# Two transformer blocks in fp32 on one core: the first four products with w_ada move from TensorE to ScalarE and GpSimd

## The reference, cut to what matters

```python
mod = jax.nn.silu(c) @ w_ada + b_ada          # c: (1, 1024), w_ada: (1024, 3072)
shift, scale, gate = jnp.split(mod, 3, axis=-1)
h = rmsnorm(x, norm_g) * (1 + scale[:, None, :]) + shift[:, None, :]
```

## Time and profile before

| what | value |
|---|---|
| median of 3 runs | 1005.55 us |
| the profiled execution | 1005.98 us, span of its core 1004.2 us |
| PE busy | 909.9 us (91%) |
| DVE, ACT, POOL busy | 362.0, 321.0, 116.9 us |
| moved by DMA | 308.62 MB, mean 307 GB/s |
| granted TensorE clock | 0.967 of full speed on average |

### The profile page before, as it was taken

One profiled execution on the slowest core, in us unless ns is written; L12 is line 12 of the kernel. 1 busy time (PEld: TensorE's weight loads), 2 busy tenths in 40 slices (PEclk: granted clock), 3 DMA queues, 4 the chain that ended last, 5 costly groups with the idle time before them and its releaser, 6 DMA issues.

```text
span 1004.2 us, 26158 instructions
## 1 busy us (share of the span) xinstructions
PE 909.9 (91%) x12047; PEld 788.9 (79%) x12047; DVE 362.0 (36%) x740; ACT 321.0 (32%) x554; POOL 116.9 (12%) x78
## 2 busy tenths in 40 slices
PE   7999999999989898987878777779999999999997
PEld 7887789977767676765656556569989999999995
DVE  4356356843111111111111111125334344873475
ACT  5546646631000000000000000125346555554443
POOL 2110021000000000000000000003311112341122
PEclk9999999999999998999899988899999999999998
DMA  8995296899999999999999999999554444455101
GB/s 283 382 348 187 95 347 231 344 426 404 403 426 424 425 424 425 424 424 426 425 425 426 426 426 424 424 357 369 200 213 168 164 175 169 169 184 202 57 1 43
DMA packets 70861, 308.62 MB, mean 307 GB/s; under 512 B 5152, under 2 KB 11728, under 8 KB 58584
## 3 DMA queue, kind: packets, MB, share of 16 engines
q1 hardware_dynamic: 66816, 302.08, 75.7%
q10 hardware_dynamic: 3928, 4.80, 1.4%
HBM read 305.81 MB, written 2.63 MB: 307 GB/s over the span
## 4 chain that ended last, share of the span: by engine, by line
PE 67%; DMA 20%; DVE 4%; issue 3%; ACT 2%; SPq 2%; POOL 1%; another core or an unknown queue 1%; POOLq 0%; DVEq 0%; ACTq 0%
PE bank L789 66%; DMA ring<-in_w 10%; DMA arena<-in_w 10%; SPq L854 2%; DVE arena L1352 1%; DVE wR L1346 1%; DMA ring<-in_w_in 1%; PE bank L1011 1%; DVE arena L1349 1%; POOL wR L2272 1%; DVE arena L1346 0%; ACT wR L1918 0%; DVE hTR L1352 0%; DVE hTR L1346 0%
## 5 line engine op out<-in xcount | busy, mean ns | idle before, releaser
L789 PE MATMUL bank<-hTR,wR 128*128 128x256 f32 x2520 | 314.3, 285 | 4.3 <-DVE hTR L1352 1.6
L789 PE MATMUL bank<-arena 128*32 128x128 f32 (+7 forms) x4378 | 277.9, 324 | 43.2 <-DMA arena<-in_w 27.3
L789 PEld LDWEIGHTS bank<-hTR,wR 128*128 128x128 f32 x2520 | 305.4, 192 | 8.3 <-issue 4.2
L789 PEld LDWEIGHTS bank<-arena 128*32 128x32 f32 (+5 forms) x4378 | 211.2, 142 | 97.7 <-issue 66.6
L1346 DVE TENSOR_TENSOR wR<-ring,wR 128x1024 fp32r<-128x1024 f32 x108 | 136.9, 1274 | 118.0 <-ACT wR L1918 117.7
L1918 ACT ACTIVATE wR<-ring 128x1024 fp32r<-128x1024 f32 x137 | 143.3, 1054 | 91.0 <-PE bank L789 88.3
L789 PE MATMUL bank<-ring,arena 128*32 128x128 f32 (+3 forms) x2352 | 103.7, 319 | 30.9 <-DMA ring<-in_w 22.0
L789 PEld LDWEIGHTS bank<-ring,arena 128*32 128x32 f32 (+1 forms) x2352 | 68.9, 114 | 51.0 <-issue 31.5
L2063 ACT ACTIVATE arena<-bank,small 128x256 f32<-128x256 f32 x32 | 15.1, 473 | 272.2 <-PE bank L789 272.2
L2272 POOL TENSOR_TENSOR wR<-ring,wR 128x1024 fp32r<-128x1024 f32 x29 | 70.7, 2437 | 265.9 <-ACT wR L1918 265.9
L1680 DVE COPY arena<-bank 128x256 f32<-128x256 f32 x32 | 13.6, 425 | 193.4 <-PE bank L789 193.4
(11 more groups left out here) (190 smaller groups left out, 669.3 us busy)
## 6 DMA issues: line engine op xcount, KB each, us to landing
arena<-in_w SPq DMA_DIRECT2D x53, 2048.0 KB, 39.6
ring<-in_w SPq DMA_DIRECT2D x42, 2048.0 KB, 40.1
ring<-in_w_in SPq DMA_DIRECT2D x25, 2048.0 KB, 10.3
ring<-in_w_ada SPq DMA_DIRECT2D x5, 2048.0 KB, 11.2
arena<-in_w_in SPq DMA_DIRECT2D x4, 2048.0 KB, 13.1
ring<-in_w_o_attn SPq DMA_DIRECT2D x2, 2048.0 KB, 8.3
ring<-in_w_out SPq DMA_DIRECT2D x2, 2048.0 KB, 7.9
ring<-in_w_in SPq DMA_DIRECT2D x2, 1024.0 KB, 9.0
```

The source lines that it names most:

```text
L789: return pe.e.matmul(o, l, r, start=start, stop=stop)
```

## The change

For ada0 to ada3 the product is taken apart. ACT multiplies each of the 8 row blocks [128, 512] of a chunk in the ring by its per-partition value of `silu(c)` in place (`ada_scale`, two blocks a step, four steps a chunk). POOL adds the 8 scaled blocks in place, 8 to 4 to 2 to 1 (`ada_add`: three adds of 1024 columns, one of 512 into ACC). PE is left with the sum over partitions (`adac_sum`: 4 matmuls of 128 weight columns with one column of ones), and DVE copies 4 columns. The four matmul steps leave the generator, which now yields 28 times; a wrapper, `with_ada`, appends scale steps after fill steps 4 to 19, adds after steps 8 to 23, sums after steps 13, 17, 21 and 25. A slot is released when its sum in ACC is written (semaphore `adac`). ada4 and ada5 stay as they were.

```diff
@@ fill_first
             for g in range(4):
-                if g in (1, 2):
-                    b = PB.use(("adaw", g - 1), PR.next()).bank
-                    for m in (1, 0):
-                        O1.add("ada", g - 1, m)
-                        yield
-                    for m in (1, 0):
-                        O1.loads.release(f"ada{2 * g - 2 + m}")
                 for c2 in range(2):
...
-                            if c2 == 0 and g in (1, 2):
-                                PB.use(("ada", g - 1), b)
-                                O1.add("ada_sum", g - 1)
                             yield
...
+        def with_ada(tiles):
+
+            for i, _ in enumerate(tiles):
+                if 4 <= i < 20:
+                    O1.add("ada_scale", i // 4 - 1, i % 4)
+                if 8 <= i < 24:
+                    O1.add("ada_add", i // 4 - 2, i % 4)
+                    if i % 4 == 3:
+                        O1.loads.release(f"ada{i // 4 - 2}")
+                if i % 4 == 1 and 12 < i < 28:
+                    PB.use(("adac", i // 4 - 3), PR.next())
+                    O1.add("adac_sum", i // 4 - 3)
+                yield
+
-        fill = fill_first()
+        fill = with_ada(fill_first())
@@ released
+            elif nm in ("ada4", "ada5"):
+                filled(e, U_["adaw", 2])
             elif nm[:3] == "ada":
-                filled(e, U_["adaw", int(nm[3]) // 2])
+                e.wait_ge(s_adac, int(nm[3]) + 1)
@@ PE
+            elif what == "adac_sum":
+                u = U_["adac", a[0]]
+                may_write(pe, u)
+                pe.wait_ge(s_adac, a[0] + 1)
+                for c in range(4):
+                    last = mm(pe, banks[u.bank][:, c:c + 1], ACC[:, 128 * c:128 * c + 128], ones[:, 0:1], True, True)
+                last.then_inc(u.full, 1)
@@ ACT
+                elif what == "ada_scale":
+                    i, part = a
+                    w = view(f"ada{i}")
+                    s.wait_ge(*landed[f"ada{i}"])
+                    s.wait_ge(s_siluc, 1)
+                    for k in (2 * part, 2 * part + 1):
+                        eng.activation(w[:, k, :], w[:, k, :], ACT.Copy, scale=sc0[:, k:k + 1]).then_inc(s_adas, 1)
@@ POOL
+                elif what == "ada_add":
+                    i, part = a
+                    w = view(f"ada{i}")
+                    p.settle()
+                    if part == 3:
+                        if i:
+                            filled(p, U_["adac", i - 1])
+                        eng.tensor_tensor(ACC, w[:, 0, :], w[:, 1, :], ALU.add).then_inc(s_adac, 1)
+                    else:
+                        o, x = ((0, 4), (2, 6), (0, 2))[part]
+                        p.wait_ge(s_adas, 8 * i + (6, 8, 8)[part])
+                        p.step(eng.tensor_tensor(flat2(w, o), flat2(w, o), flat2(w, x), ALU.add))
```

More of the change, by code:

```diff
@@ L1505, in first_steps @@
                         ALU.subtract).then_inc(u.free, 1)
-                elif what == "ada_sum":
+                elif what == "adac_sum":
                     if a[0] == 0:
@@ L1509, in first_steps @@
                         tt(wr[:, :, :], wr[:, :, :], bc(col[:, 24:32], 36), ALU.mult).then_inc(s_wg, 1)
-                    ada_columns(a[0])
+                    u = U_["adac", a[0]]
+                    filled(v, u)
+                    eng.tensor_copy(abr[:, 4 * a[0]:4 * a[0] + 4], banks[u.bank][:, 0:4]).then_inc(u.free, 1)
                 elif what == "y_sum":
```

21 lines of the change are left out of this document (6 added, 15 removed).

## The result

| | before | changed |
|---|---|---|
| device time, median (range), us | 1005.68 (1005.25 to 1007.03, 4 runs) | 1018.88 (1017.53 to 1022.06, 4 runs) |
| profiled execution: its time / span, us | 1005.98 / 1004.2 | 1019.86 / 1018.1 |
| mean granted clock of TensorE | 0.967 | 0.954 |

The ratio is 1.0132, 95% interval 1.0116 to 1.0148: the change makes the kernel 13.2 us slower. Forecast were 1006.5 us and a range up to 1011.5, so the time lies 12.4 us above the forecast and outside the range.

What follows compares the result with a forecast made beforehand. The attention's end, which releases the first expert load and the full DMA stream behind it, was taken as the bound. Terms -5.6 + 2.3 + 0.6 + 3.6 = +0.9 us gave 1006.5 us, range 1001.5 to 1011.5.

Steps and rivals of the forecast that it cites:

- the term on POOL: Attention loop: POOL's adds make DVE operations wait 1.2 us on average, mostly covered; +0.6 us, bounds 0 and +5.
- Rival B: Attention: DVE and POOL exclude each other, so PE waits at the transposes; +5 to +6 over forecast, 1011.5 us; chance 0.20.
- PE, -5.6: PE in the attention: 8.9 us of work removed, 3.3 us of sums added; net -5.6 us if nothing else waits.
- ACT, +2.3: ACT's scalings in the attention delay normalization: stalls 0.3 us at i = 6, 2.0 at i = 8; range 0 to +6.
- Tail, +3.6: Attention's end: four fill steps fewer to cover the last heads, stalls of 0.6, 1.7 and 1.3 us; range 0 to +5.
- Chain of the end: First expert load waits for the attention's last low part; any shift there moves the load stream and the end equally.
- Slots and loads, 0: Ring slots of ada0 to ada3 come free no later than their loads are wanted; cost 0.
- Rival A: Attention: ACT's and DVE's idle time absorbs the new work, only the tail costs; 1000 to 1003.5, say 1002 us; chance 0.22.
- C: Rival: the change is hidden, the expert stream sets the end and its first issue stays; 1005.6 us; chance 0.08.
- the main theory: Follow-up experiments: DVE's two-SBUF-operand operations and small TENSOR_SCALAR wait for POOL's running add, delaying softmax, PE and expert loads.

Runs made afterwards that it cites:

- experiment 6: Changed kernel with the 128x288 router weight scaling moved to a step ahead of the attention; 1015.74 us, ratio 1.0096 to the kernel before.
- experiment 4: Changed kernel with fill steps left out at i = 10, 12 and 14, so the fill lasts to i = 15; 1022.40 us, ratio 1.016.
- Experiment 12: Changed kernel without long adds, scalings cut to 8 columns, missing fill steps left out at i = 1, 3, 5, 7, not the end; 1001.15 us, ratio 0.9939.
- experiment 1: Changed kernel without POOL's twelve adds of 1024 columns, scalings kept; 1007.59 us, ratio 1.0011 to the kernel before.
- 3: Changed kernel without the twelve long adds and with scalings cut to 8 of 512 columns; 1005.48 us, ratio 0.9994.
- Experiment 7: Changed kernel with extra identity matmuls on PE at four places where it stood idle; 1018.29 us, ratio 1.0122.
- 9: Changed kernel with the router weights scaled ahead of the attention and each 1024-column add split into two of 512; 1013.40 us, ratio 1.0088.
- 11: Changed kernel without long adds, scalings cut to 8 columns, missing fill steps left out at i = 10, 12, 14, not the end; 1004.79 us, ratio 0.9983.
- 2: Changed kernel with each of ACT's 32 scalings cut to 8 of 512 columns, adds kept; 1013.59 us, ratio 1.0071.
- 13: Changed kernel in full, with the four missing fill steps left out at i = 1, 3, 5, 7, not at the end; 1025.68 us, ratio 1.0208.
- 14: Changed kernel with early router scaling, halved adds, and missing fill steps left out at i = 1, 3, 5, 7, not the end; 1016.46 us, ratio 1.0111.
- 8: Changed kernel with every 1024-column add on POOL split into two of 512; 1017.09 us, ratio 1.0104.
- experiment 15: Changed kernel with each of the twelve long POOL adds replaced by a 1024-column multiplication by 1; 1013.70 us, ratio 1.0066.
- experiment 5: Changed kernel with the sixteen adds on DVE instead of POOL, at the same places; 1015.65 us, ratio 1.009.
- experiment 10: Changed kernel with no scaling on ACT and no add on POOL, DVE doing eight 512-column operations per product; 1019.66 us, ratio 1.0139.

## Why the prediction was wrong

**The step that failed** is the term on POOL: "For the rest of the loop ... I take +0.6; bounds 0 and +5 (two waits of 2.4 that nothing covers)". The twelve long adds measured 11.3 us with ACT's scalings and 8.1 without (12.2 and 7.7 by the ratios). The mechanism was named with its row, and Rival B built on it, at 1011.5 with a chance of 0.20. It came true in kind and at more than twice its price (+12.4 over the forecast, not +5 to +6). Three things were missing:

- The mean. "Waits 1.2 us on average" and DVE at 80% were weighed against PE's distance in tiles. From 89 to 145 us POOL was busy 62% of the time (forecast 60%), and DVE 59% (49% before), far from 80%. The loss came from coincidences: the low part and the router scaling each waited out an add, 4.2 us ahead of one transpose (experiment 6: 3.1 us for the router scaling alone). The change moved that scaling from `ada_sum` 0 (at 125.17 before, 0.45 us) to `adac_sum` 0, among the adds; I priced it at nothing.
- The direction. I thought of DVE as the only one held. POOL's adds were held too, 2.32 to 3.20 us, so POOL took 40 us, not 34, and its norms, which stand behind the adds in its order, came late: DVE was idle 3.56 us for one at 155.89 and 7.45 in experiment 4, where it was 2.73 without the long adds. The prediction asked where a low part is wanted, not where the norm is.
- Where it decides: "over 0.5 us at each of the twelve transposes". It was 4.58 us at one transpose and 2.40 at one fill tile, whose own low part was late, though the prediction gave low parts two tiles (over 6 us) of room. The other two long waits, 1.90 at `p_turn` 10 and 1.33 at a `diff_out`, belong to the tail's term: without the long adds they were 1.39 and 1.70.

**PE, -5.6.** Not contradicted. A sum costs 0.88 (108.18 to 109.06) or 0.81 (147.77 to 148.58). Experiment 12, in which no transpose waits, reached 1001.15 with the small scalings left in; that is 5.2 under the median of the kernel before in that comparison (6.1 by the ratio, 4.4 to 7.7), and its first load came 3.6 earlier.

**ACT, +2.3.** Measured 2.1 (experiments 1 and 3). The places were wrong: in the kernel without adds `p_turn` 5, at i = 6, waited 1.43 (forecast 0.3) and the one at i = 8 0.53 (forecast 2.0). A pair took 1.33 us, or 1.23 from start to start, not 1.1. With the adds the scalings cost 5.3; the sum had nothing for that.

**Tail, +3.6.** In the kernel without adds the three waits were 1.39, 1.70 and 1.18 (forecast 0.6, 1.7 and 1.3): 4.3. By experiment 12 the missing cover costs 4.3. Sum of the three terms: +0.3 forecast, +1.1 measured in experiment 1 (its ratio; -0.2 to +2.4). So the forecast was good for the kernel without its long adds, the places of ACT's waits apart.

**Chain of the end.** The load moved by 12.55 and the end by 13.9, so the end moved with it, as argued, and by 1.4 more. **Clock.** The prediction had no term for it; three tiles were slow, with a clock of 0.50, behind waits of 4.58, 2.40 and 1.33 (after 1.90). Experiments 6 and 7 price them at an estimated 1.5 to 2 us. **Slots and loads, 0.** Nothing in the rows contradicts it. **Rival A and C** are excluded by the waits and by the load's time. Of the fifteen expectations the main theory's range held in three (3, 6, 9), and a rival's in two (7, 11). Among those that failed, 2, 4, 13 and 14 treated the terms as separate, and 8 the adds' price as proportional to their length.

## What to carry to other kernels

Before work goes to an engine that is "11% busy", look in the trace for an operation there that stretched another engine's, count what of the other engine's work falls under the new operations, and ask at each place what the two or three operations ahead of the critical one would do if each waited out a whole one. Idle share says little about room in a loop whose engines take their work in written order: here the long adds on POOL (twelve of 2.4 us) cost 11.3 us, 25 us of work on DVE 14, and 21 us on ACT 5.3 beside the adds and 2.1 without them. Price edits at the corners (neither, one, the other, both), since the terms of such a loop don't add up.

## What the runs showed of the hardware

- DVE and POOL exclude each other both ways, in part of their operations. DVE's two-operand SBUF work (1.23 to 3.31 us; 0.45 to 2.59) and even its 128x2 `TENSOR_SCALAR` (0.17 to 1.52) end late by what is left of POOL's running two-operand operation. DVE's operations that read PSUM did not (420 and 417 ns), nor did its 128x2 `RECIPROCAL` (0.15 at 114.33, inside an add). POOL's add of 1024 columns grew from 2.32 to 3.20 when it met DVE.
- Under a multiplication of 1024 columns by a constant on POOL (one operand from SBUF, 2.77 us alone) DVE was held for the first 0.89 us only, in five of five cases; a low part that met it later took 1.22. The Trainium skill (GPSIMD Engine Reference, Key points) names DVE's side of the contention, the 2-port modes and two SBUF inputs; experiment 15 adds that what POOL runs sets how long DVE is held.
- On DVE, `TENSOR_TENSOR` takes 1.22 us for 128x1024 and 0.69 for 128x512 (experiment 5), and `SCALAR_TENSOR_TENSOR` of 128x512 0.75 (experiment 10): half the columns are not half the time.
- TensorE ran at 0.50 of full clock from 116 to 119 us, behind 4.58 us without work. Experiment 7 filled about half of that gap and of the two behind it: the clock was 0.50 again behind the first (118 to 121 us) and stayed at 1.00 behind the others. A wait of 1.32 us was followed by a tile of 3.11 us in one kernel and of 4.59 in another (experiments 8 and 9).
